# Expert norm rows turned without their root, and idle products in TensorE's waits, in a two-layer hybrid trunk

## The reference, cut to what matters

```python
for layer in range(2):
    h = rmsnorm(x, norm_mix[layer])
    y = even_mixer(h, ...) if layer == 0 else conv_mixer(h, ...)   # 4 mLSTM + 4 differential-attention heads / gated conv3
    x = x + y
    h = rmsnorm(x, norm_ffn[layer])
    x = x + hier_moe(h, ...)
return rmsnorm(x, norm_final)

def rmsnorm(x, g):
    return x * rsqrt(mean(x * x, -1) + 1e-6) * g

def hier_moe(t, wg, bg, we, be, w_gate, w_up, w_down):
    glog, elog = t @ wg + bg, t @ we + be      # 4 groups, 4 experts in each
    # top-1 group, top-2 experts within it; weights: softmax of the two, times the group's probability
    for e in range(16):
        out += combine[:, e] * ((silu(t @ w_gate[e]) * (t @ w_up[e])) @ w_down[e])
```

## Time and profile before

| | us |
|---|---|
| median of 3 runs (range) | 1180.72 (1178.05 to 1180.93) |
| the profiled execution | 1180.17 |
| its span, first to last instruction | 1178.3 |
| TensorE busy | 1105.9 (94%) |
| VectorE busy | 891.4 (76%) |
| ScalarE busy | 648.6 (55%) |
| GpSimd busy | 119.0 (10%) |
| mean granted TensorE clock | 0.963 |

### The profile page before, as it was taken

How to read it: one execution, slowest core, us unless ns; L and a number is a source line. 1 busy time by engine, 2 the same in 40 slices (tenths; PEclk the granted TensorE clock), 3 DMA queues, 4 the chain that set the end, 5 groups by cost and what they waited for, 6 DMA issues and landing times.

```text
span 1178.3 us, 15323 instructions
## 1 busy us (share of the span) xinstructions
PE 1105.9 (94%) x5404; PEld 835.9 (71%) x5404; DVE 891.4 (76%) x1133; ACT 648.6 (55%) x809; POOL 119.0 (10%) x160
## 2 busy tenths in 40 slices
PE   5999999789999999999998899999999999999994
PEld 4776767557777777777775888878877777777772
DVE  5244546877678999999998562454688999999987
ACT  5123444422247888888885221232357888888872
POOL 3000000021110200000003100000111000000022
PEclk9999999899979999999999899999979999999997
DMA  8632222130249999999998433233159999999984
GB/s 309 188 134 72 81 81 72 40 121 1 72 137 342 374 397 393 409 398 398 409 414 312 176 107 107 72 108 107 72 183 355 391 407 397 396 395 410 405 313 167
DMA packets 77604, 286.41 MB, mean 243 GB/s; under 512 B 16648, under 2 KB 16648, under 8 KB 61165
## 3 DMA queue, kind: packets, MB, share of 16 engines
q1 hardware_dynamic: 65212, 241.64, 54.0%
q0 software_dynamic: 8608, 30.95, 8.0%
q10 hardware_dynamic: 3728, 13.11, 2.8%
HBM read 266.79 MB, written 20.20 MB: 244 GB/s over the span
## 4 chain that ended last, share of the span: by engine, by line
PE 83%; DVE 10%; ACT 3%; issue 2%; DMA 1%; POOL 1%; POOLq 0%; SPq 0%; ACTq 0%; DVEq 0%; PEldq 0%
PE ps L1680 25%; PE ps L1682 24%; PE ps L1681 24%; DVE w_split L964 2%; PE ps L2009 1%; ACT w_split L622 1%; DVE arena L985 1%; DVE arena L1330 1%; PE ps L1767 1%; PE ps L1925 1%; DVE arena L1158 1%; PE ps L1662 1%; PE ps L2033 1%; PE ps L1881 1%; PE ps L1946 1%
## 5 line engine op out<-in xcount | busy, mean ns | idle before, releaser
L964 DVE TENSOR_TENSOR w_split<-ring,w_split 128x1024 fp32r<-128x1024 f32 x452 | 540.3, 1221 | 87.4 <-ACT w_split L622 75.4
L622 ACT CAST w_split<-ring 128x1024 fp32r<-128x1024 f32 x452 | 471.4, 1052 | 189.6 <-PE ps L1682 186.7
L1680 PE MATMUL ps<-w_split,hT 128*96 128x512 f32 (+2 forms) x976 | 391.2, 401 | 11.1 <-DVE w_split L964 4.1
L1681 PE MATMUL ps<-w_split,hT 128*96 128x512 f32 (+2 forms) x976 | 383.8, 393 | 0.0
L1682 PE MATMUL ps<-w_split,hT 128*96 128x512 f32 (+2 forms) x976 | 383.7, 393 | 0.0
L1680 PEld LDWEIGHTS ps<-w_split,hT 128*96 128x96 f32 (+1 forms) x976 | 165.8, 170 | 75.3 <-issue 14.7
L1682 PEld LDWEIGHTS ps<-w_split,hT 128*96 128x96 f32 (+1 forms) x976 | 165.5, 170 | 61.4
L1681 PEld LDWEIGHTS ps<-w_split,hT 128*96 128x96 f32 (+1 forms) x976 | 166.0, 170 | 55.2 <-issue 0.3
L1680 PE MATMUL ps<-hT,w_split 128*128 128x512 f32 (+1 forms) x384 | 147.4, 384 | 6.4 <-issue 4.6
L1681 PE MATMUL ps<-hT,w_split 128*128 128x512 f32 (+1 forms) x384 | 144.8, 377 | 0.0
L1682 PE MATMUL ps<-hT,w_split 128*128 128x512 f32 (+1 forms) x384 | 144.7, 377 | 0.0
(11 more groups left out here) (244 smaller groups left out, 869.1 us busy)
## 6 DMA issues: line engine op xcount, KB each, us to landing
ring<-in_exp_w_gate SPq DMA_DIRECT2D x64, 1024.0 KB, 10.3
ring<-in_exp_w_up SPq DMA_DIRECT2D x64, 1024.0 KB, 10.0
ring<-in_exp_w_down SPq DMA_DIRECT2D x64, 1024.0 KB, 11.8
ring<-in_w_in_even SPq DMA_DIRECT2D x14, 1024.0 KB, 12.0
y_rows_dram<-arena ACTq DMA_DIRECT2D x32, 384.0 KB, 7.0
ring<-in_w_in_odd SPq DMA_DIRECT2D x12, 1024.0 KB, 5.3
ring<-in_w_out_even SPq DMA_DIRECT2D x4, 1024.0 KB, 4.9
h_rows_dram<-arena POOLq DMA_DIRECT2D x8, 512.0 KB, 4.3
```

What stands on the lines that cost most here:

```text
L622: s.copy(hi_of(c), raw(c)).then_inc(hi_ready, 1)
L964: v.tensor_tensor(lo_of(c), raw(c), hi_of(c).bitcast(F32), ALU.subtract).then_inc(lo_ready, 1)
L1680: mm(out, a[0], b[0], start=start, stop=False)
L1681: mm(out, a[1], b[0], start=False, stop=False)
```

## The change

It does three things.
- Expert norm rows: `h_rows` of the two expert norms holds x times the gain, without the root (`gained`, by halves of 512 columns). The root is applied to the logits in `route_pair` and `route_tile`, and to the rows by ScalarE (`scale_row`) once they are turned; the first gather and the store to DRAM wait for that (`row_scaled`). The orders of the router are new on all engines.
- Idle products: `keep_busy(n, bank)` issues n products of 128 x 512 in fp16 into a bank whose content isn't needed.
- Orders: two of the four turnings of an attention head's output go into the middle of the next projection; in the last expert `result_weights` goes ahead of the copy of the first half; `last_rows` begins with half of the result; at the odd entrance the low part of tile 1 goes ahead of two splits.

```diff
                 for t in range(TT):
-                    pool.wait_ge(h_ready, (2 * l + 1) * TT + t + 1)
+                    pool.wait_ge(row_scaled, TT * l + t + 1)
                     pool.dma_start(h_dram[t * P:(t + 1) * P, :], h_rows[:, t, :]).then_inc(h_stored, 16)
...
+            def mixer_norm(l, weights):
+                n = 2 * l + 1
+                def scale_row(t):
+                    act.wait_ge(norm_rstd, n * TT + t + 1)
+                    s.activation(h_rows[:, t, :], h_rows[:, t, :], ACT.Copy, scale=st[:, 4 + t:5 + t]).then_inc(row_scaled, 1)
+                square(n, 0)
+                square(n, 1)
+                copy_turned(n, 0)
+                if l:
+                    square(n, 2)
+                copy_turned(n, 1)
+                if l == 0:
+                    square(n, 2)
+                scale_row(0)
+                scale_row(1)
+                copy_turned(n, 2)
+                square(n, 3)
+                weights()
+                copy_turned(n, 3)
+                scale_row(2)
+                scale_row(3)
...
             for step in range(UNITS + 1):
                 if step < UNITS:
                     soft(step)
+                    if step in (8, 12):
+                        scale_out((step - 8) // TT)
...
-                if step >= 7 and (step - 7) % TT == 0:
-                    scale_out((step - 7) // TT)
+                if step == 15:
+                    scale_out(2)
...
+            def gained(n, t, half):
+                if t == 0 and half == 0:
+                    dve.wait_ge(gain_loaded, 16 * n)
+                if half:
+                    dve.wait_ge(x_ready, (n - 1) * TT + t + 1)
+                cs, places = slice(half * 512, half * 512 + 512), slice(half * 64, half * 64 + 64)
+                row, gains = (a.rearrange("q (p k) -> q p k", k=KD) for a in (x_sb[:, t, cs], gain[:, cs]))
+                ins = v.tensor_tensor(h_rows[:, t, :].rearrange("q (k p) -> q p k", k=KD)[:, places, :], row, gains, ALU.mult)
+                if half:
+                    ins.then_inc(h_ready, 1)
...
-                link(v.tensor_tensor(lg[:, t, :], ps[:, LOGIT_BANK[t], t * NR:(t + 1) * NR], b_route[:, l, :], ALU.add))
+                dve.wait_ge(norm_rstd, (2 * l + 1) * TT + t + 1)
+                link(v.scalar_tensor_tensor(out=lg[:, t, :], in0=ps[:, LOGIT_BANK[t], t * NR:(t + 1) * NR], scalar=st[:, 4 + t:5 + t],
+                                            in1=b_route[:, l, :], op0=ALU.mult, op1=ALU.add))
...
-                        scaled(n, t)
+                        for half in range(2):
+                            gained(n, t, half)
                     for half in range(2):
                         add_output(0, half, 2)
                     splits(step_chunk(l, 0) + 2)
...
-                    scaled(n, 2)
+                    for half in range(2):
+                        gained(n, 2, half)
                     add_output(0, 0, 3)
+                    gained(n, 3, 0)
...
                     for t in range(TT):
                         add_output(l, 0, t)
+                        gained(n, t, 0)
...
                         add_output(l, 1, t)
-                        scaled(n, t)
+                        gained(n, t, 1)
                 route_pair(l)
                 add_output(l, 1, 3)
+                gained(n, 3, 1)
                 place_pair(l)
-                for g in range(2):
-                    select(g, (0, 1))
-                scaled(n, 3)
                 route_tile(l, 2)
                 place_tile(l, 2)
                 splits(step_chunk(l, 0) + 3)
                 route_tile(l, 3)
                 place_tile(l, 3)
-                select(0, (2, 3)).then_inc(sel_ready, 1)
+                select(0, range(TT)).then_inc(sel_ready, 1)
...
-                select(1, (2, 3)).then_inc(sel_ready, 1)
+                select(1, range(TT)).then_inc(sel_ready, 1)
...
                 last_hidden(l, n, c, 0)
-                splits(c + 15)
+                result_weights(l)
                 copy_last_actT(l, n, 0)
                 splits(c + 16)
                 last_hidden(l, n, c, 1)
-                result_weights(l)
                 copy_last_actT(l, n, 1)
...
             scaled(2, 1)
             low_part(2, 0)
+            splits(PIECE * ODD_BASE + 2)
+            low_part(2, 1)
             splits(PIECE * ODD_BASE + 4)
-            low_part(2, 1)
...
+            def keep_busy(n, bank):
+                for _ in range(n):
+                    mm(ps[:, bank, :], ones16[:, :], later[:, 0:1].broadcast_to([P, 512]), start=True, stop=True)
             pe.wait_ge(consts_ready, 8)
+            keep_busy(20, 7)
             for t in range(TT - 1):
                 turn_h(0, t)
+            keep_busy(12, 7)
...
+            keep_busy(11, 3)
...
-                    all_jobs([EARLY + step])
+                    behind = (step - 8) // TT if step in (8, 12) else None
+                    job(EARLY + step, None if behind is None else lambda k: turn_out(behind) if k == 4 else None)
+                if step == UNITS:
+                    keep_busy(6, 2)
...
-                if step >= 7 and (step - 7) % TT == 0:
+                if step == 15:
+                    keep_busy(12, 2)
+                if step in (15, 19):
                     turn_out((step - 7) // TT)
...
-                pe.wait_ge(m_normed, h + 1)
                 if h:
                     pe.wait_ge(m_cat, h)
+                    keep_busy(6, 4)
+                pe.wait_ge(m_normed, h + 1)
...
+                def gather_first(t, ks=range(KD)):
+                    if t == 0 and ks[0] == 0:
                         for b in (5, 6):
                             mm(ps[:, b, :], ones16[:, :], later[:, 0:1].broadcast_to([P, 512]), start=True, stop=False)
                     pe.wait_ge(first_sel_ready, TT * l + t + 1)
-                    for k in range(KD):
+                    pe.wait_ge(row_scaled, TT * l + t + 1)
+                    for k in ks:
                         ins = mm(ps[:, 5 + k // 4, (k % 4) * P:(k % 4) * P + CAP], h_rows[:, t, k * P:(k + 1) * P], sel_first[:, t, :],
                                   start=False, stop=(t == TT - 1 and k % 4 == 3))
...
+                    keep_busy(9, 6)
...
                     first_logits()
+                    turn_h(n, 2)
...
-                    tile(1, 3, midway=first_logits)
-                turn_h(n, 2)
+                    tile(1, 3, midway=(first_logits, lambda: turn_h(n, 2)))
+                logits(2)
                 ranks(0)
                 ranks(1)
-                gather_first(0)
-                logits(2)
                 turn_h(n, 3)
+                gather_first(0, range(0, 4))
+                logits(3)
+                ranks(2)
+                gather_first(0, range(4, KD))
                 gather_first(1)
-                ranks(2)
-                logits(3)
-                gather_first(2)
+                gather_first(2, range(0, 4))
                 ranks(3)
                 for r in range(TT):
                     last = mm(ps[:, 7, RANK0:RANK0 + E], ones16[:, :], member[:, r, :],
                               start=(r == 0), stop=(r == TT - 1))
                 last.then_inc(rank_full, 1)
+                keep_busy(2, 0)
+                gather_first(2, range(4, KD))
                 gather_first(3)
                 slot_index(l, 0)
...
+                keep_busy(4, 0)
                 pe.wait_ge(y_half0, E * (l + 1))
-                pe.wait_ge(y_half1, E * (l + 1))
                 for t in range(TT):
                     for half in range(2):
+                        if t == 0 and half:
+                            pe.wait_ge(y_half1, E * (l + 1))
...
             turn_h(2, 0)
+            keep_busy(5, 4)
             turn_h(2, 1)
+            keep_busy(9, 4)
```

More of the change, by code:

```diff
@@ new lines, in square, with norm @@
+            def square(n, t):
+                if n == 0:
+                    act.wait_ge(x_loaded[t], 16)
+                else:
+                    act.wait_ge(x_ready, (n - 1) * TT + t + 1)
+                if n or t:
+                    act.wait_ge(sumsq_ready, n * TT + t)
+                s.activation(junk, x_sb[:, t, :], ACT.Square, accum_out=st[:, t:t + 1]).then_inc(sumsq_ready, 1)
+            def norm(n, copies=True):
+                for t in range(TT):
+                    square(n, t)
+                    if copies and t and n:
+                        if t == TT - 1:
+                            copy_turned(n, t - 1)
+                        elif t == 1:
+                            copy_turned(n, 0)
+                            copy_turned(n, 1)
@@ L938, in _ @@
             splits(at_start(p + 1))
-            norm(3, behind_last=lambda: splits(at_start(p + 2)))
+            mixer_norm(1, lambda: splits(at_start(p + 2)))
             experts(1)
@@ L1242, in add_output @@
                     total, rest = ps[:, j, :], x_sb[:, t, cs]
```

(6 more changed lines are left out.)

72 lines of the change are left out of this document (26 added, 46 removed).

## The result

The changed kernel takes 1169.48 us in the median of 5 runs (1166.74 to 1173.28) against 1180.72 (1178.05 to 1182.4): a ratio of 0.991, interval 0.9893 to 0.9926. The profiled execution took 1169.08, its span is 1166.9 against 1178.3, 11.4 less, and the mean granted clock is 0.982 against 0.963.

The account below looks back on a forecast made before the run. The prediction took TensorE as the bound (83% of the chain that ended last, VectorE 10%). Its terms summed to 6.3 us off 1180.2, giving 1173.9, stated as 1174.0; own range 1170 to 1178 (chance 0.44), wide range 1164 to 1181.

Parts of the forecast that it names:

- Start: Kernel start: 20 idle products hidden before the first transposes, 12 more behind them; 1.4 us gained, -0.2 if the clock falls.
- Gate columns: TensorE's 2.56 us wait until 97.41: 11 idle products hidden there keep the following products fast; 1.3 us gained.
- Attention: Turnings of attention heads' outputs: two waits of 2.0 us and the slow stretches behind them go; 6.6 us gained, bounds 4.0 to 7.
- Heads: mLSTM heads: six idle products ahead of each wait stick out at third and fourth, 1.3 us each; 2.6 us lost.
- Router, layer 0: First router: ranks 2.3 us earlier, 2.7 lost in a slow last gather, 1.0 less 0.6 lost to moved selects; -0.8 us.
- rival A: Both layers' routers run at 2.4 GHz: +3.3 and +0.2 us for -0.8 and -3.5, so 1166 us; chance 0.22.
- Router, layer 1: Second router: tile 3's copy waits behind four casts, ranks 0.4 us later, then 2.7 and 1.0-0.6 lost; -3.5 us.
- Last expert: Last expert of each layer: TensorE starts 1.9 us earlier, second half ends 0.6 earlier, last rows 0.5 more; 1.15 us gained, twice.
- Odd entrance: Odd entrance: tile 1 starts 2.3 us earlier, then TensorE waits for tile 2; 1.6 us gained, bounds 0.2 to 2.6.

## Why the prediction was right, point by point
The time lay in the wide range (1164 to 1181) and the sign was right, but it was just below the forecast's own 1170 to 1178: the sum of 6.3 us was 5.1 short of the spans' 11.4. The routers were mis-sized by 4.7 and 2.6, and attention over-counted by 1.4. In the routers this is a balance with luck in it: the clock was better by 6.1 and 5.8 us than the sum had it, and other terms were worse by 1.4 and 3.3.

- **Start.** 0.9 instead of 1.4. The step said that 20 products take 4.3 us and end at 8.7, on the word of a granted clock of 1.00. They took 6.85, to 11.2, and pushed the first transposes by 1.39, which the spaces gave back. Here the Trainium skill (TensorE: Matmul & The Clock Gate, "Part 1: The HAM clock gate"), whose default state is the throttled one, was right and my reading of the row wrong: 16 first transposes took 3.63 us cold and 1.91 behind the idle products. The 20 cost nothing and bring nothing.
- **Gate columns.** 1.6 for 1.3; without idle products it is gone.
- **Attention.** 7.4 up to the third head for 6.6, all of it from the order (7.6 alone). The third head's part held: the fourth is turned 13.40 us behind it with the 12 and 6 idle products and without. The step failed where it let the gain stand to the end: TensorE now waits 4.41 instead of 0.36 for the fourth head and its clock falls to 0.58 for 11 us, so it is 21.88 us to the first mLSTM head instead of 19.60 and 2.3 are given back. Net 5.2. Nine other profiles with this order and no filler there lose 0.8 to 1.8, so part of the 2.3 is chance.
- **Heads.** -2.7 for -2.6, and shown by taking them out.
- **Router, layer 0.** 3.9 gained for 0.8 lost, the largest miss. The stage from the first tile's turning to the second expert's hidden rows (74.90 us, then 71.02) splits in four.
  - To the fourth tile's ranks 2.9 are gained, for 2.3. The five other profiles with the same selections gain 1.3 to 2.3.
  - From there to the first index product 1.1 are gained (4.29 us, then 3.21), for 2.7 lost. The step took what stands there as slow, an idle pair and 24 records in 0.86 and 5.6 us; they took 0.4 and 2.81, as in rival A. That as many small products would keep the clock low was only argued, and it failed: it is 2.9 to 3.2 us in all eleven profiles with the new router, 2.86 without any idle product. A slow stretch came earlier instead, in the first gathers (32 records in 5.42).
  - From there to the turning of the second expert's tokens 2.3 are gained (12.28 us, then 10.00). The step, and rival A too, had this at nothing, though the earlier trace rows show the low clock up to 350.5: with 1.00 behind the router the first expert's products run fast.
  - In the rest 2.4 are lost, for 1.0 less 0.6. The selections moved behind make TensorE wait 2.52 for the second expert's tokens, with a slow clock behind; moving one of them brought 3.5.
- **Router, layer 1.** -0.9 for -3.5, in the same four parts: 1.7 lost for 0.4, 1.1 gained for 2.7 lost, 2.0 gained for nothing, 2.4 lost for 0.4. The copy behind four casts, TensorE idle in front of it, and the low clock came as forecast; the low clock lay in the logits and the first gathers (3.5 us each) instead of the last, and was over before the last ones. Copying first brought 4.1 in the stage.
- **Last expert.** 1.2 and 0.9 for 1.15 each. TensorE starts at once (617.89), as forecast.
- **Odd entrance.** 1.3 for 1.6: the chain moved to tile 2, with a wait of 2.92 where about 3 was said. The idle products there bring nothing: without them the third tile is turned at the same 648.82.

## What to carry to other kernels
An idle product can pay only in a wait that it fits (18 in the wait for the fourth attention head kept the clock at 1.00 in three profiles of three), and costs its full length where the engine has no wait: place each by the wait of its own row. When a row's work is moved out of a planned place, look for who then waits in the queue that it moved to: here one selection of 1.96 us and one copy behind casts cost 6.5 and 5.7 us by the ratios. All idle products together bring 3.8, which isn't clear of noise, and one order in attention 6.8. Read a gain of a few us from the same instruction in two traces, and let the medians of several runs say whether it stays.

## What the runs showed of the hardware
- With identical instructions the clock falls in different places: 254 to 260 us ran at 1.00 in one kernel's profile and 0.72 in another's whose edit lies 580 us later. The runs of one kernel spread over up to 9.4 us, those of the kernel before over 2.7 to 6.6.
- The granted clock of a row can read 1.00 at the start while the products run slow: 20 of them 6.85 us, 12 of the same form 10 us later 2.77.
- In the second router, from tile 3's turning to the first index product: 16.3 to 18.2 us in seven profiles with the copy behind the casts, 13.1 to 14.7 in four with the copy first; in the first router 12.8 to 14.7 in the eleven profiles with its new order.
- What TensorE did in the router decided the clock at which the first expert begins: over the 7 us from the first index product on it was 0.50 to 0.66 in three profiles with the router as before and 1.00 in eleven with the new one, in both layers, with and without idle products.
